# Expert weights of a mixture-of-experts step in 4 MB instead of 2 MB transfers

## Chip, core and metric

The kernel runs on one core of one Trainium2 chip. The metric is the device time of one execution in microseconds (us); the median of several executions is compared. MB in the names of transfers stands for 1,024 KB; the profile's GB/s are powers of ten.

## What is computed

One layer of a hybrid decoder on 272 prompt tokens (16 of them learned) and 8 decode tokens: a Mamba-2 group and a convolution group share an input and an output projection, and a top-4-of-32 expert block follows. Only the expert block matters here. All is float32. Cut to this part:

```python
logits = (xf @ w_router + b_router).astype(F32)
top_val, top_idx = lax.top_k(logits, TOP_K)                # 4 of 32 experts per token
gates = jax.nn.softmax(top_val, axis=-1).astype(u.dtype)
...
def expert_rows(args):
    xblk, e = args
    gt = jnp.minimum(xblk @ w_gate[e] + b_gate[e], SWIGLU_LIMIT)
    up = jnp.clip(xblk @ w_up[e] + b_up[e], -SWIGLU_LIMIT, SWIGLU_LIMIT)
    hdn = (up + 1.0) * gt * jax.nn.sigmoid(gt * SWIGLU_ALPHA)
    return hdn @ w_down[e] + b_down[e]
```

Each of `w_gate[e]`, `w_up[e]` and `w_down[e]` is 1024 x 1024 float32, 4 MB; an expert has 12 MB, the 32 experts 384 MB, and each matrix is read once. The expert block serves 264 tokens with 4 experts each, so an expert has 33 tokens in the mean.

## The kernel before

The first 286 us or so do everything ahead of the experts. Then the 32 experts are worked through in an order found at run time by their token counts: experts 0 and 1 in straight code, 2 to 31 in a loop of 15 rounds, each with a **big** and a **small** expert (`big_expert`, `small_expert`). In this text an expert's number is its place in that order; the even ones are big, the odd ones small. A big expert puts 64 tokens across TensorE's columns (line 1447, matmuls of 128 x 64 by 512), a small one has at most 32 tokens, four groups of columns (line 1490, by 256). A big expert with more than 64 tokens is done in two halves (`by_width` picks `what(2)`), so that each product is made twice; such an expert is called **wide** here.

The weights lie in a ring in SBUF of 12 pieces (`ring`, `piece(p)`), 1 MB each: pieces 0 to 3 are the gate matrix, 4 to 7 the up matrix, 8 to 11 the down matrix. The ring holds exactly one expert. On each expert TensorE goes through the pieces in this order; between them it puts the former expert's rows into the result (`scatter`, `scatter_s`), gathers the next expert's rows (`gather`, line 1424, or `gather_s`) and turns the hidden values (line 1205). Every product of a piece begins with `pe.wait_ge(landed[p // 2], i16)`: `landed` has one semaphore for each pair of pieces.

SyncE (SP) only issues transfers. The first expert's six pairs are fetched ahead (`prefetch`). Then a loop over the 31 others (lines 357 to 364) asks for pair after pair of the next expert, each as soon as TensorE has used the same pair of the present one. TensorE says so by semaphores: `gate_half` and `gate_used` for pairs 0 and 1, and `piece_used` for the others, eight counts for each expert: the fourth comes when the up matrix has been used (on a big expert by the first matmul of the gathering), the eighth at the end of the down matrix. A transfer of a pair is 128 partitions x 16 KB. All requests stand in one queue and are served in their order.

On a big expert of one width `gate_half` and `gate_used` both come with the first matmuls of piece 4; on a wide one after pieces 1 and 3 of the second half; on a small one after piece 1 and with the first matmul of piece 4.

Of the kernel before, what the change touches and what calls it, by code (L numbers as in the profile page):

```python
# [47 lines left out]
def build(nc, I, O):  # L48
    ctx = ExitStack()
    with ctx:  # L50
        def sb(name, n, dt=F32):
            return ctx.enter_context(nc.sbuf_tensor(name, [P, n], dt))

        def sem(name):
            return ctx.enter_context(nc.semaphore(name))

        def view(t, off, *dims):
            n = 1
            for d in dims:
                n *= d  # L60
            a = t[:, off:off + n]
            if len(dims) == 1:
                return a
            names = "abc"[:len(dims)]
            return a.rearrange("p (" + " ".join(names) + ") -> p " + " ".join(names),
                               **dict(zip(names, dims)))
# [12 lines left out]
        PIECE = 2 * D  # L79
        NP = 12  # L80
        ring = sb("ring", NP * PIECE)
# [131 lines left out]
        ev = {n: sem(n) for n in names}  # L213
        landed = [sem(f"pair_landed{i}") for i in range(NP // 2)]
# [28 lines left out]
        def piece(p):  # L243
            return view(ring, p * PIECE, 2, D)

        def pair_row(q):
            return view(ring, 2 * q * PIECE, 2 * PIECE)
# [4 lines left out]
        expert_w = I["w_experts"]  # L252

        def expert_pair(e, q):
            return expert_w[bass.ds(e, 1), q].rearrange("o p n -> p (o n)")

        tok = [(0, P), (P, P), (2 * P, NB)]

        NR = CW - 1
# [6 lines left out]
        def _(sp):  # L266
# [89 lines left out]
            sp.wait_ge(ev["order_ready"], 1)  # L356
            with sp.Fori(0, NE - 1) as i:
                e = sp.value_load(order[0:1, bass.ds(i + 2, 1)], min_val=0, max_val=NE - 1)
                for q in range(2):
                    sp.wait_ge(ev[("gate_half", "gate_used")[q]], i + 1)  # L360
                    sp.dma_start(pair_row(q), expert_pair(e, q)).then_inc(landed[q], 16)
                for q in range(2, NP // 2):
                    sp.wait_ge(ev["piece_used"], i * 8 + 2 * q - 2)
                    sp.dma_start(pair_row(q), expert_pair(e, q)).then_inc(landed[q], 16)

            sp.wait_ge(ev["o_tab"], 1)
            n_over = sp.value_load(otab[0:1, OVER:OVER + 1], min_val=0, max_val=OVER)
            with sp.If(n_over > 0):
                sp.wait_ge(ev["o_list"], 1)
                with sp.Fori(0, OVER) as j:  # L370
                    with sp.If(j < n_over):
                        e = sp.value_load(otab[0:1, bass.ds(j, 1)], min_val=0, max_val=NE - 1)
                        sp.wait_ge(ev["piece_used"], j * 8 + NE * 8)
                        for q in range(NP // 2):
                            sp.dma_start(pair_row(q), expert_pair(e, q)).then_inc(landed[q], 16)
            for q in range(4):
                sp.wait_ge(ev["f_ready"], 2 * q + 2)
                sp.dma_start(O["y_t"][:, 2 * TN * q:2 * TN * (q + 1)], flat(yo[:, 2 * q:2 * q + 2, :])).then_inc(ev["f_out"], 16)
# [821 lines left out]
        def _(pe):  # L1200
# [214 lines left out]
            def halves(bank):  # L1415

                return [ps[HALF * h:HALF * (h + 1), bank, :] for h in range(2)]
# [17 lines left out]
            def bias(bank, row):  # L1435
                for h_, dst in enumerate(halves(bank)):
                    MM(dst, oh[row:row + NE, :], brow[row:row + NE, 512 * h_:512 * (h_ + 1)],  # L1437
                       start=True, stop=False, skip_group_check=True)

            def piece_products(p, b, src, bank, fresh, i16):  # L1440
                pe.wait_ge(landed[p // 2], i16)
                hs = []
                for k in range(2):
                    kk = 2 * (p % 4) + k
                    o = 512 * b + P * (kk % 4) + HALF * (kk // 4)
                    for h_, dst in enumerate(halves(bank + b)):
                        hs.append(MM(dst, src[:, o:o + HALF], piece(p)[:, k, 512 * h_:512 * (h_ + 1)],  # L1447
                                     start=(fresh and kk == 0), stop=(kk == KT - 1), skip_group_check=True))
                return hs
# [11 lines left out]
            def quarters(bank):  # L1461

                return [ps[QUAR * q:QUAR * (q + 1), bank, 0:256] for q in range(4)]
# [17 lines left out]
                       start=False, stop=False, skip_group_check=True)  # L1481

            def piece_products_s(p, src, bank, fresh, i16):
                pe.wait_ge(landed[p // 2], i16)
                hs = []
                for k in range(2):
                    kk = 2 * (p % 4) + k
                    o = P * (kk % 2) + QUAR * (kk // 2)
                    for q, dst in enumerate(quarters(bank)):
                        hs.append(MM(dst, src[:, o:o + QUAR], piece(p)[:, k, 256 * q:256 * (q + 1)],  # L1490
                                     start=(fresh and kk == 0), stop=(kk == KT - 1), skip_group_check=True))
                return hs
# [71 lines left out]
            def gate_of(n, i16, then):  # L1564
                for p in range(4):
                    hs = piece_products(p, 0, xT, 0, False, i16)
                    if p == 3:
                        hs[-1].then_inc(ev["gate_done"], 1)
                    then(n, p)

            def up_of(n, i16):
                if n == 1:
                    for p in range(4, 8):
                        hs = piece_products(p, 0, xT, 2, False, i16)
                        if p == 4:
                            hs[0].then_inc(ev["gate_half"], 1)
                            hs[1].then_inc(ev["gate_used"], 1)
                        hs[-1].then_inc(ev["up_first" if p == 7 else "piece_used"], 1)
                else:
                    bias(1, 64)  # L1580
                    bias(3, 96)
                    for p in range(4):
                        hs = piece_products(p, 1, xT, 0, False, i16)
                        if p % 2:
                            hs[-1].then_inc(ev[("gate_half", "gate_used")[p // 2]], 1)
                    for p in range(4, 8):
                        hs = piece_products(p, 0, xT, 2, False, i16)
                    hs[-1].then_inc(ev["up_first"], 1)
                    for p in range(4, 8):
                        hs = piece_products(p, 1, xT, 2, False, i16)  # L1590
                        if p < 7:
                            hs[-1].then_inc(ev["piece_used"], 1)
# [19 lines left out]
            def gate_s(i16, then):  # L1612
                for p in range(4):
                    hs = piece_products_s(p, xT, 0, True, i16)
                    if p == 0:
                        bias_s(0, 64)
                    if p == 1:
                        hs[-1].then_inc(ev["gate_half"], 1)
                    if p == 3:
                        hs[-1].then_inc(ev["gate_done"], 1)  # L1620
                    then(p)

            def up_s(i16):
                for p in range(4, 8):
                    hs = piece_products_s(p, xT, 2, True, i16)
                    if p == 4:
                        hs[0].then_inc(ev["gate_used"], 1)
                        bias_s(2, 96)
                    hs[-1].then_inc(ev["piece_used"], 1)

            def down_s(i2, i16):
                pe.wait_ge(ev["ht_ready"], i2 + 2)
                pe.wait_ge(ev["xg_out"], i2 + 3)
                for p in range(8, NP):
                    hs = piece_products_s(p, hT_e, 4, True, i16)
                    hs[-1].then_inc(ev["piece_used"], 1)
# [69 lines left out]
            for m in range(4):  # L1706
                if m == 3:
                    pe.wait_ge(ev["acc_done"], NE * 4 + 1)
                for h_ in range(2):
                    q = m // 2 + 2 * h_  # L1710
# [91 lines left out]
```

## Time and profile before

| | |
|---|---|
| median of 3 runs | 1286.16 us (1285.48 to 1294.58) |
| the profiled execution | 1288.3 us, span 1286.5 us |
| TensorE matmul busy | 1173.8 us, 91% of the span |
| VectorE, ScalarE busy | 485.5 us, 195.5 us |
| mean granted TensorE clock | 0.964 of full |
| transfers | 451.33 MB, mean 351 GB/s over the span |
| weights in the loop and ahead of it | 192 transfers of 2,048 KB |

The span is cut into 40 slices of 32.2 us in the page's second part; its DMA row gives the mean busy share of the 16 DMA engines. In a timeline a row is a run of like instructions: start, length, engine, line, operation, tiles, shapes, count, and in brackets the idle time ahead of it with what ended it. SPq rows are the moments at which SP issues a transfer, not the transfer.

### The profile page before, as it was taken

To read this page: it belongs to the slowest core of one execution; us is meant where nothing else is said; L and a number is where in the kernel's file an instruction comes from. 1 tells how busy PE (TensorE), PEld (TensorE's weight loads), DVE (VectorE), ACT (ScalarE), POOL (GpSimd) and SP (SyncE) were. 2 spreads that over 40 slices of the span, in tenths; PEclk is the share of its full clock that TensorE was granted. 3 is DMA by queue.
4 is the path that set the end of the run, shared out by engine and by line. 5 is a ranking of instruction groups with operands and counts; after the bars stand their busy time and mean duration, and the time that the engine had idled before them with its cause. 6 is when DMAs were issued, how large, how long until landed. Compare 5 with 4: busy or idle time off the path is not lost.

```text
span 1286.5 us, 21155 instructions
## 1 busy us (share of the span) xinstructions
PE 1173.8 (91%) x8454; PEld 551.2 (43%) x8455; DVE 485.5 (38%) x1078; ACT 195.5 (15%) x431; POOL 4.6 (0%) x28
## 2 busy tenths in 40 slices
PE   7999989997988989999989999799998887989886
PEld 5888768873333233433333433233432322333323
DVE  2799998114432322232312233222233332323233
ACT  1234504021110110111101111100111111011012
POOL 0000000000000000000000000000000000000000
PEclk9999998997999989999989999999999999899897
DMA  9452329623999999899999899998999999999993
GB/s 396 165 208 74 139 104 318 264 74 120 381 425 427 428 427 408 329 420 431 428 428 419 329 428 429 428 428 357 393 422 428 428 428 430 426 430 427 429 428 149
DMA packets 36994, 451.33 MB, mean 351 GB/s; under 512 B 5112, under 2 KB 5656, under 8 KB 10080
## 3 DMA queue, kind: packets, MB, share of 16 engines
q1 hardware_dynamic: 35344, 449.02, 84.0%
q10 hardware_dynamic: 1616, 1.82, 0.4%
q8 instruction: 25, 0.41, 0.1%
q14 instruction: 9, 0.07, 0.0%
HBM read 443.57 MB, written 7.25 MB: 350 GB/s over the span
## 4 chain that ended last, share of the span: by engine, by line
PE 55%; DMA 30%; DVE 12%; issue 1%; DVEq 1%; ACT 0%; SPq 0%; ACTq 0%
DMA ring<-in_w_experts 29%; PE ps L1447 24%; PE ps L1490 8%; DVE acts L713 5%; PE ps L1229 3%; PE ps L1331 2%; PE ps L1424 2%; PE ps L1388 2%; PE ps L1499 2%; PE ps L1457 2%; PE ps L1205 2%; DVE acts L808 1%; PE ps L1322 1%; PE ps L1437 1%; PE ps L1480 1%
## 5 line engine op out<-in xcount | busy, mean ns | idle before, releaser
L1447 PE MATMUL ps<-ring,extra 128*64 128x512 f32 x1824 | 426.3, 613 | 15.3 <-DMA ring<-in_w_experts 15.3
L1068 DVE TENSOR_TENSOR acts<-ps,acts 128x528 f32<-128x528 f32 x128 | 90.6, 708 | 409.4 <-PE ps L1499 207.0
L1447 PEld LDWEIGHTS ps<-ring,extra 128*64 128x64 f32 x1824 | 124.3, 139 | 268.6 <-issue 235.3
L1490 PE MATMUL ps<-ring,extra 128*32 128x256 f32 x3072 | 203.3, 400 | 39.3 <-DMA ring<-in_w_experts 39.3
L1490 PEld LDWEIGHTS ps<-ring,extra 128*32 128x32 f32 x3072 | 89.8, 113 | 142.3 <-DMA ring<-in_w_experts 58.7
L713 DVE SCALAR_TENSOR_TENSOR acts<-acts,small 128x256 f32<-128x256 f32 x224 | 91.3, 477 | 0.7 <-ACT acts L453 0.7
L1229 PE MATMUL ps<-acts,ring 128*128 128x280 f32 (+1 forms) x320 | 75.3, 395 | 0.3 <-ACT ring L524 0.3
L1229 PEld LDWEIGHTS ps<-acts,ring 128*128 128x128 f32 x320 | 60.6, 190 | 14.0 <-issue 1.0
L1229 PE MATMUL ps<-acts,extra 128*128 128x280 f32 x256 | 64.2, 415 | 1.9 <-DVE acts L695 1.9
L1082 DVE TENSOR_SCALAR extra<-ps 128x512 f32<-128x512 f32 x32 | 22.0, 688 | 97.8 <-PE ps L1447 82.5
L1229 PEld LDWEIGHTS ps<-acts,extra 128*128 128x128 f32 x256 | 50.6, 198 | 14.9 <-issue 2.3
L604 ACT ACTIVATE extra<-extra 128x512 f32<-128x512 f32 x32 | 19.7, 630 | 243.7 <-DVE extra L1073 243.7
L1424 PE MATMUL ps<-acts 128*64 128x512 f32 (+1 forms) x228 | 56.6, 616 | 0.0
L1205 PE MATMUL ps<-small,extra 128*128 128x128 f32 x220 | 39.0, 290 | 14.4 <-DVE extra L1087 13.0
L1457 PE MATMUL ps<-acts,extra 64*128 64x264 f32 x304 | 51.2, 427 | 0.0
L1499 PE MATMUL ps<-acts,extra 32*128 32x264 f32 x256 | 46.7, 442 | 0.0
L1105 DVE SCALAR_TENSOR_TENSOR acts<-ps,acts 128x264 f32<-128x264 f32 x48 | 22.2, 490 | 63.3 <-ACT acts L634 63.2
L1205 PEld LDWEIGHTS ps<-small,extra 128*128 128x128 f32 x220 | 22.8, 140 | 48.6 <-issue 20.8
L1499 PEld LDWEIGHTS ps<-acts,extra 32*128 32x128 f32 x256 | 19.6, 187 | 55.8 <-issue 55.8
L599 ACT ACTIVATE extra<-ps 128x512 f32<-128x512 f32 x34 | 20.4, 600 | 144.5 <-PE ps L1424 134.2
L1055 DVE TENSOR_SCALAR extra<-ps 128x256 f32<-128x256 f32 x16 | 6.8, 425 | 83.7 <-PE ps L1490 83.7
L614 ACT ACTIVATE extra<-ps 128x512 f32<-128x512 f32 x32 | 17.4, 594 | 132.8 <-PE ps L1447 132.8
(290 smaller groups left out, 883.3 us busy)
## 6 DMA issues: line engine op xcount, KB each, us to landing
ring<-in_w_experts SPq DMA_DIRECT2D x192, 2048.0 KB, 22.1
ring<-in_w_in_t SPq DMA_DIRECT2D x5, 2048.0 KB, 20.8
extra<-in_w_in_t SPq DMA_DIRECT2D x4, 2048.0 KB, 9.3
extra<-in_w_out_t SPq DMA_DIRECT2D x4, 1024.0 KB, 5.9
ring<-in_w_out_t SPq DMA_DIRECT2D x4, 1024.0 KB, 5.8
ring<-in_state_t SPq DMA_DIRECT2D x8, 512.0 KB, 6.9
ring<-dtx_rows SPq DMA_DIRECT2D x8, 512.0 KB, 5.8
out_ssm_s_t<-ring SPq DMA_DIRECT2D x8, 512.0 KB, 4.1
```

The source lines that it names most:

```text
L713: STT(conv[:, m, 0:SEQ], cbuf[:, m, k:k + SEQ], cw[:, m, k:k + 1], conv[:, m, 0:SEQ], ALU.mult, ALU.add).then_inc(ev["tap_added"], 1)
L1068: TT(both, ps[:, 6:8, 0:TN], both, ALU.add).then_inc(ev["acc_done"], 1)
L1105: return STT(Pm[:, bank, :], ps[:, 6, 0:TN], slot_id[:, slot:slot + 1], gp, ALU.is_equal, ALU.mult)
L1205: return nc.tensor.transpose(out, in_, ident[0:r, 0:r])
L1229: h = MM(ps[:, tile_bank(j), 0:T - lo], win(c)[:, k, P * q:P * (q + 1)], uT[:, k, lo:T], start=(k == 0), stop=(k == KT - 1))
L1331: h = MM(ps[:, m, 0:TN], wout(4 + k // 2)[:, k % 2, P * m:P * (m + 1)], conv[:, k, :], start=(k == 0), stop=False, skip_group_check=True)
L1388: h = MM(ps[:, m, 0:TN], wout(k // 2)[:, k % 2, P * m:P * (m + 1)], yT[:, k, :], start=False, stop=(k == KT - 1), skip_group_check=True)
L1424: h = MM(dst, S[0:r, j, HALF * b:HALF * (b + 1)], xn[0:r, j, 512 * h_:512 * (h_ + 1)], start=(j == 0), stop=(j == 2))
L1447: hs.append(MM(dst, src[:, o:o + HALF], piece(p)[:, k, 512 * h_:512 * (h_ + 1)], start=(fresh and kk == 0), stop=(kk == KT - 1), skip_grou ...
L1457: h = MM(ps[:, 6 + h_, 0:TN], ys[rows, 512 * b + P * m:512 * b + P * (m + 1)], Pm[rows, b, :], start=(b == 0), stop=(b == n - 1))
L1490: hs.append(MM(dst, src[:, o:o + QUAR], piece(p)[:, k, 256 * q:256 * (q + 1)], start=(fresh and kk == 0), stop=(kk == KT - 1), skip_group_ ...
L1499: h = MM(ps[:, 6 + h_, 0:TN], ys[QUAR * q:QUAR * (q + 1), P * (m % 2):P * (m % 2 + 1)], Pm[QUAR * q:QUAR * (q + 1), 0, :], start=True, sto ...
```

## The change

The loop on SP asks for a whole matrix: one transfer of 128 partitions x 2 x 16 KB in place of two of 128 x 16 KB. The gate matrix is asked for at `gate_used`, the up matrix at the fourth and the down matrix at the eighth count of `piece_used`. The semaphore of the matrix's second pair (`landed[1]`, `landed[3]`, `landed[5]`) counts its landing, and TensorE waits for it ahead of the matrix's first piece only (`p % 4 == 0`). The first expert, fetched ahead by pairs as before, is still waited for by pairs. The overflow loop, which runs only if an expert's tokens don't fit, is changed in the same way; it is not entered with this data.

```diff
+        def matrix_rows(t):
+            return ring[:, 4 * t * PIECE:4 * (t + 1) * PIECE].rearrange("p (q n) -> p q n", q=2)
+
+        def expert_matrix(e, t):
+            return expert_w[bass.ds(e, 1), 2 * t:2 * t + 2].rearrange("o q p n -> p (o q) n")
...
                 e = sp.value_load(order[0:1, bass.ds(i + 2, 1)], min_val=0, max_val=NE - 1)
-                for q in range(2):
-                    sp.wait_ge(ev[("gate_half", "gate_used")[q]], i + 1)
-                    sp.dma_start(pair_row(q), expert_pair(e, q)).then_inc(landed[q], 16)
-                for q in range(2, NP // 2):
-                    sp.wait_ge(ev["piece_used"], i * 8 + 2 * q - 2)
-                    sp.dma_start(pair_row(q), expert_pair(e, q)).then_inc(landed[q], 16)
+                sp.wait_ge(ev["gate_used"], i + 1)
+                sp.dma_start(matrix_rows(0), expert_matrix(e, 0)).then_inc(landed[1], 16)
+                for t in range(1, 3):
+                    sp.wait_ge(ev["piece_used"], i * 8 + 4 * t)
+                    sp.dma_start(matrix_rows(t), expert_matrix(e, t)).then_inc(landed[2 * t + 1], 16)
...
+            def matrix_here(p, i16):
+                if isinstance(i16, int) and i16 == 16:
+                    pe.wait_ge(landed[p // 2], 16)
+                elif p % 4 == 0:
+                    pe.wait_ge(landed[p // 4 * 2 + 1], i16)
+
             def piece_products(p, b, src, bank, fresh, i16):
-                pe.wait_ge(landed[p // 2], i16)
+                matrix_here(p, i16)
```

`piece_products_s` changes like `piece_products`. The order of SP's instructions in one round of its loop, before (line 361 asks for pairs 0 and 1, line 364 for pairs 2 to 5):

```order
56 L361 ISA [waits gate_half]
57 L361 DMA ring<-in_w_experts 128x4096
58 L361 ISA [waits gate_used]
59 L361 DMA ring<-in_w_experts 128x4096
60 L363 ISA
61 L364 ISA [waits piece_used]
62 L364 DMA ring<-in_w_experts 128x4096
63 L363 REGISTER_ALU
64 L364 ISA [waits piece_used]
65 L364 DMA ring<-in_w_experts 128x4096
```

(and two more such requests behind these), and with the change (line 366 asks for the gate matrix, line 369 for the other two):

```order
56 L366 ISA [waits gate_used]
57 L366 DMA ring<-in_w_experts 128x2x4096
58 L368 ISA
59 L369 ISA [waits piece_used]
60 L369 DMA ring<-in_w_experts 128x2x4096
61 L368 REGISTER_ALU
62 L369 ISA [waits piece_used]
63 L369 DMA ring<-in_w_experts 128x2x4096
```

Six requests with a wait each have become three; the wait on `gate_half` is gone and pair 0 goes with pair 1.

On TensorE, the start of the small expert in the loop, before (line 1490 are its products, 1480 its biases, 1457 the former expert's rows; `pair_landed0` to `pair_landed5` are the semaphores in `landed`):

```order
358 L1490 MATMUL ps<-ring,extra 32x256 [waits pair_landed0]
359 L1490 MATMUL ps<-ring,extra 32x256 x7
360 L1480 MATMUL ps<-acts 32x256 x4
361 L1457 MATMUL ps<-acts,extra 128x264 [waits y_back,p_ready]
362 L1457 MATMUL ps<-acts,extra 128x264
363 L1490 MATMUL ps<-ring,extra 32x256 [waits pair_landed0]
364 L1490 MATMUL ps<-ring,extra 32x256 x7
365 L1457 MATMUL ps<-acts,extra 128x264 [waits acc_done]
366 L1457 MATMUL ps<-acts,extra 128x264
367 L1490 MATMUL ps<-ring,extra 32x256 [waits pair_landed1]
368 L1490 MATMUL ps<-ring,extra 32x256 x7
```

and with the change (the same lines are 1501, 1491 and 1468 there):

```order
358 L1501 MATMUL ps<-ring,extra 32x256 [waits pair_landed1]
359 L1501 MATMUL ps<-ring,extra 32x256 x7
360 L1491 MATMUL ps<-acts 32x256 x4
361 L1468 MATMUL ps<-acts,extra 128x264 [waits y_back,p_ready]
362 L1468 MATMUL ps<-acts,extra 128x264
363 L1501 MATMUL ps<-ring,extra 32x256 x8
364 L1468 MATMUL ps<-acts,extra 128x264 [waits acc_done]
365 L1468 MATMUL ps<-acts,extra 128x264
366 L1501 MATMUL ps<-ring,extra 32x256 x8
```

No matmul has moved; the wait for the second pair now stands ahead of the first piece, and the waits inside the matrix are gone.

## Rows read from the trace of the kernel before

**Rows 1.** The page, chain that ended last, by line.

```profile
DMA ring<-in_w_experts 29%; PE ps L1447 24%; PE ps L1490 8%; DVE acts L713 5%; PE ps L1229 3%; PE ps L1331 2%; PE ps L1424 2%; PE ps L1388 2%; PE ps L1499 2%; PE ps L1457 2%; PE ps L1205 2%; DVE acts L808 1%; PE ps L1322 1%; PE ps L1437 1%; PE ps L1480 1%
```

**Rows 2.** The page: GB/s by slice; issues with count, KB, us to landing.

```profile
GB/s 396 165 208 74 139 104 318 264 74 120 381 425 427 428 427 408 329 420 431 428 428 419 329 428 429 428 428 357 393 422 428 428 428 430 426 430 427 429 428 149
...
ring<-in_w_experts SPq DMA_DIRECT2D x192, 2048.0 KB, 22.1
```

**Rows 3.** Windows: length, busy PE PEld DVE ACT POOL, clock, DMA share, GB/s.

```profile
689.80:737.30 47.50, 46.78 (x388) 18.52 (x388) 12.01 (x25) 5.11 (x11) 0.00 (x0) 1.00 0.89 354
...
606.60:665.30 58.70, 52.51 (x404) 18.79 (x408) 17.00 (x34) 6.23 (x13) 0.00 (x0) 0.94 1.01 429
```

**Rows 4.** Timeline, experts 10 and 11; last, a request on SP and its landing.

```profile
606.66 1.94 PE L1447 MATMUL ps<-ring,extra 128*64 128x512 f32 x8 [0.63 <-DMA ring<-in_w_experts]
...
640.93 1.07 PE L1490 MATMUL ps<-ring,extra 128*32 128x256 f32 x16 [0.97 <-DMA ring<-in_w_experts]
...
636.22 0.33 SPq L364 DMA_DIRECT2D ring<-in_w_experts  x1
...
DMA to landing us min/median/max: 24.3/24.3/24.3
```

**Rows 5.** Timeline of TensorE around the wide experts (6, 12, 18).

```profile
494.44 20.82 PE L1447 MATMUL ps<-ring,extra 128*64 128x512 f32 x96
...
667.88 1.94 PE L1447 MATMUL ps<-ring,extra 128*64 128x512 f32 x8
...
735.73 3.66 PE L1490 MATMUL ps<-ring,extra 128*32 128x256 f32 x64
...
741.10 1.94 PE L1447 MATMUL ps<-ring,extra 128*64 128x512 f32 x8
...
863.29 20.82 PE L1447 MATMUL ps<-ring,extra 128*64 128x512 f32 x96
```

**Rows 6.** SP's requests around expert 12; a landing time belongs to the row above.

```profile
646.62 0.33 SPq L361 DMA_DIRECT2D ring<-in_w_experts  x1
...
DMA to landing us min/median/max: 23.6/23.6/23.6
...
666.37 0.33 SPq L364 DMA_DIRECT2D ring<-in_w_experts  x1
...
DMA to landing us min/median/max: 23.5/23.5/23.5
...
686.22 0.33 SPq L361 DMA_DIRECT2D ring<-in_w_experts  x1
...
700.48 0.33 SPq L364 DMA_DIRECT2D ring<-in_w_experts  x1
...
718.32 0.33 SPq L364 DMA_DIRECT2D ring<-in_w_experts  x1
...
DMA to landing us min/median/max: 7.8/7.8/7.8
...
727.81 0.33 SPq L361 DMA_DIRECT2D ring<-in_w_experts  x1
...
DMA to landing us min/median/max: 9.4/9.4/9.4
```

**Rows 7.** Timeline, last expert: TensorE; last request on SP and its landing.

```profile
1255.29 3.43 PE L1490 MATMUL ps<-ring,extra 128*32 128x256 f32 x32 [2.26 <-DMA ring<-in_w_experts]
...
1263.08 3.90 PE L1490 MATMUL ps<-ring,extra 128*32 128x256 f32 x64
...
1240.81 0.33 SPq L364 DMA_DIRECT2D ring<-in_w_experts  x1
...
DMA to landing us min/median/max: 24.2/24.2/24.2
```

**Rows 8.** The loop's first two requests on SP and the landings of the two.

```profile
323.33 0.94 SPq L361 DMA_DIRECT2D ring<-in_w_experts  x2
...
DMA to landing us min/median/max: 9.2/11.3/13.5
```

More of the change, by code:

```diff
@@ L373, in _ @@
                         sp.wait_ge(ev["piece_used"], j * 8 + NE * 8)
-                        for q in range(NP // 2):
-                            sp.dma_start(pair_row(q), expert_pair(e, q)).then_inc(landed[q], 16)
+                        for t in range(3):
+                            sp.dma_start(matrix_rows(t), expert_matrix(e, t)).then_inc(landed[2 * t + 1], 16)
             for q in range(4):
@@ L1483, in piece_products_s @@
             def piece_products_s(p, src, bank, fresh, i16):
-                pe.wait_ge(landed[p // 2], i16)
+                matrix_here(p, i16)
                 hs = []
```

## The prediction, made before the changed kernel ran

> **What bounds the kernel now.** I read the page's chain first, to see who ends the span. Its two largest parts are the wait for expert weights and the products that use them [rows 1]. The reader is to see that both stand side by side: the kernel is neither plainly transfer-bound nor plainly TensorE-bound. The page's slices and its table of issues come next [rows 2]: from the twelfth slice to the last but one the transfers run at 419 GB/s or more, except for three dents (408 and 329, 329, 357 and 393). There are 192 weight transfers of 2,048 KB, and a median of 22.1 us passes from request to landing, although 2 MB at 428 GB/s take 4.9 us. So most requests stand in a queue behind some 17 us of other transfers.
>
> The windows tell the two sorts of stretch apart [rows 3]. From 606.60 to 665.30, one big and one small expert, the 16 DMA engines are busy for the whole time at 429 GB/s and TensorE for 52.5 of 58.7 us: here the transfers set the pace. From 689.80 to 737.30 the rate is 354 GB/s, while TensorE is busy for 46.8 of 47.5 us: here TensorE sets it and the queue runs dry. The timeline of TensorE says why [rows 4, 5]. In a steady pair it waits before piece 0 of a big expert (606.66, 0.63 us) and before pairs of the small one (640.93, 0.97 us). An expert with more than 64 tokens takes every product twice; its row is the run of 96 matmul instructions of 20.82 us, and there are three such rows, the first at 494.44, the second at 678.94, the last at 863.29. These three wide experts (6, 12 and 18 in the order of use) make the three dents. Behind each, the transfers catch up, and TensorE waits for weights again before the next one comes (606.66 lies between the first and the second). From then on the transfers set the pace: **what the DMA engines lose around a wide expert is lost for the whole kernel.**
>
> **What the change does there.** The ring holds exactly one expert, so a transfer can start only where something was used up. The 12 MB come in three requests instead of six. The bytes, the 16 KB runs and the matmul instructions stay. Two things get coarser: a matrix is requested when its last pair is free (the first pair waits for the second), and its first product waits for 4 MB (the first pair's user waits for the second pair too).
>
> **Steady stretches cost nothing.** A 4 MB transfer takes 9.8 us. TensorE starts a matrix up to 4.9 us later than now, but then finds all of it. The gate matrix of expert 12 is the tightest to follow: its second pair is requested at 646.62 [rows 6], so at 651.5 at the latest after the change. It is needed when expert 11's last pair has landed, 636.22 + 24.3 = 660.5 [rows 4]. That is 9.0 us ahead, and a request needs 2.9 us of its own with no transfer in front of it (7.8 - 4.9, the request at 718.32 [rows 6]). So the queue does not run dry. The fewer DMA instructions on SP and fewer waits on TensorE are worth nothing here: each SP issue takes 0.33 us behind a queue of 17 us. Of cover there is 9.0 - 2.9 = 6.1 us; a stall beyond this would be lost in each pair.
>
> **Around a wide expert it costs 7.3 us.** I follow expert 12. TensorE starts it at 667.88 [rows 5] while the second gate pair lands at 646.62 + 23.6 = 670.2 [rows 6]; afterwards it starts at 670.3, 2.4 us later, and so do its releases. Before it, the down matrix of expert 12 lands last, at 689.9 (the request at 666.37 took 23.5 us [rows 6]). With 2.9 us from request to start on an idle queue and 9.8 us for 4 MB:
> - Gate of 13: requested at 686.22 + 2.4 = 688.6, starts at 691.5, lands at 701.3. Idle 1.6 us.
> - Up of 13: 700.48 + 2.4 = 702.9, starts at 705.8, lands at 715.6. Idle 4.5 us.
> - Down of 13: 718.32 + 2.4 = 720.7, starts at 723.6, lands at 733.4. Idle 8.0 us.
> - Gate of 14: 727.81 + 2.4 = 730.2, while another transfer runs. For such a request the rows show up to 9.4 us in all [rows 6], 4.5 above the transfer itself. By 4.5 it starts at 734.7 and lands at 744.5 (by 2.9 at 743.2).
>
> Before the change the second gate pair of 14 landed at 727.81 + 9.4 = 737.2. So the transfers are 7.3 us behind (6.0 by the lower price). The reason in a sentence: one expert's three requests fall 14 and 18 us apart here while a transfer lasts 9.8 us, so the engines idle between them, where the small requests in between used to fill in. Expert 13 does not wait for weights: it needs its down matrix at 735.73 + 2.4 = 738.1, and the matrix is there at 733.4. Expert 14 wants to begin at 741.10 + 2.4 = 743.5 [rows 5] and waits 1.0 us. The three wide experts have the same neighbours, a small one after them: 3 x 7.3 = 21.9 us.
>
> **Start and end.** The first request of the loop goes out with the second pair's (323.33, two in 0.94 us; the second pair lands 13.5 us after its own request, at 337.4 [rows 8]). One 4 MB request at 323.9 lands at 336.6: 0.8 us gained, hidden, but carried into the first transfer-bound stretch. At the end the last pair lands at 1240.81 + 24.2 = 1265.0 and the last product ends at 1263.08 + 3.90 = 1267.0 [rows 7], 2.0 us later, since two pieces were done before. With the whole down matrix landing at once, all 64 instructions come after it, 3.66 us in the row at 735.73 [rows 5]: 1.7 us lost. What follows the last expert does not change.
>
> **Sum**: 21.9 - 0.8 + 1.7 = 22.8 us. The profiled execution took 1288.3 us (span 1286.5), 2.1 above the median of 1286.16; I add the sum to the median: 1309.0 us, 1.8% slower.
>
> **A rule of the Trainium skill against the row.** In the stretch 606.60:665.30 twelve 2 MB transfers follow each other with the engines fully busy at 429 GB/s [rows 3]: a larger transfer finds nothing between transfers to save. The Trainium skill (DMA: Bandwidth & Descriptors, section Bandwidth) gives 341 GB/s for 1 MB and 425 GB/s for 16 MB, so larger requests should be faster; an estimate between them on a log scale gives 362 and 383 GB/s for 2 and 4 MB, 5.5% off some 910 us of transfers, about 50 us gained, and the sum would be near 1259 us. This trace has 2 MB at more than the page's rate for 16 MB, since its requests are queued.
>
> **Rivals.**
> 1. *Faster, by cheaper transfers.* Each transfer would have to carry a cost that the rows don't show. The change removes 93 requests of the loop; to end 1% under 1286 (12.9 us) against the 22.8 of the sum, each must give back 0.38 us of DMA time. Time at that point: 1273 us. Against it stands the full business of the engines [rows 3]. Chance 0.03.
> 2. *Within 1%, the loss is absorbed.* If TensorE set the pace from one wide expert to the next, later transfers would be covered, and start and end alone (0.9 us) would remain: 1287 us. It decides where less than 4 us per wide expert reach the steady stretches. For it speaks that TensorE is busy for 46.8 of 47.5 us behind expert 12; against it the wait at 606.66 [rows 4], and that a pair needs 52.5 us of TensorE and 58.7 of transfers. Chance 0.07.
> 3. *The 4 MB transfer is slower.* Each DMA engine would now step between two places of the same partition's data 2 MB apart. The trace shows no transfer of this shape. Of some 910 us of transfers each per cent of rate costs 9 us: 4% would give 1345 us. It is bounded from one side by the 12 transfers at 429 GB/s, which go through the same places one after the other. The Trainium skill (DMA: Bandwidth & Descriptors, section Latency and other measured facts) lists row pitches of 512 KiB at 207 GB/s and 2 MiB at 164; no row here shows it, and here the rows of one pair stay 16 KB apart. Chance 0.06.
> 4. *The clock of TensorE.* Waits become fewer and longer (up to 4.9 us more at a time), and after a wait of 2.26 us the granted clock's lower level (1.2 GHz) shows: 32 matmul instructions take 3.43 us at 1255.29, where 64 take 3.66 at 735.73 [rows 7, 5], 1.6 us lost. One such loss at the start of each wide expert and at the end gives 4 x 1.6 = 6.4 us more, 1315 us. In steady pairs two more fit into the 6.2 us that TensorE has to spare; only beyond it the pace changes hands. The Trainium skill (TensorE: Matmul & The Clock Gate, section HAM oscillation — how this bites in real kernels) describes matmuls that start cold after each wait for a transfer; the row agrees, with 3.43 us for 32. Chance 0.04 that it adds over 6 us.
>
> **How the numbers follow.** The forecast as worked out gets 0.80. Its low end: 6.0 instead of 7.3 for each wide expert (-3.9), and if TensorE enters them undelayed, because the transfers run 2.4 us further ahead by then, up to 4 us less: 1301. Its high end: the clock (+6.4) and half a per cent of transfer rate (+4.5): 1320. The range 1301 to 1320 leaves the rivals 1 to 3 out. A difference under about 1% can't be told from none for this kernel; slower by over 1% (above 1299) takes the forecast, rivals 3 and 4: 0.90; within 1% 0.07; faster 0.03.
>
> **What would show it.** In the profile after: 93 transfers of 4,096 KB beside the first expert's six of 2,048 KB, at 428 GB/s in steady stretches; the dents around the three wide experts deeper, with idle DMA stretches of about 1.6, 4.5 and 8 us; no idle DMA elsewhere in the expert stage; TensorE waiting once or twice in a matrix's place, for up to 4.4 us, and never inside a matrix; the last weights landing some 21 us later and the last product 3.7 us after them. A steady rate under 425 GB/s would prove rival 3; dents in steady stretches would mean that the 6.1 us of cover is not there; a start of the small expert behind a wide one that waits for weights would make each wide expert dearer than 7.3 us.

## The result, and the profile after

The changed kernel takes 1311.61 us in the median (1310.45 to 1321.4, 3 runs) against 1286.16 us: ratio 1.0206, 95% interval 1.0153 to 1.0259. By the medians it is slower by 25.5 us; the two profiled executions differ by 23.3 us (1311.6 and 1288.3 us; spans 1309.8 and 1286.5 us). The forecast was 1309.0, range 1301 to 1320. One execution of the run called wait below (1315.2 us) fell in a slower state of the chip and is left out of its median and ratio.

The page after, its slices (TensorE's granted clock in tenths, DMA share in tenths, GB/s) and its two kinds of weight requests:

```profile
PEclk9999998998989989999999998999998989898897
DMA  9451338622999997799998799997899999999992
GB/s 397 177 189 65 137 143 308 273 98 83 427 427 425 428 428 310 314 428 431 426 431 341 316 426 430 428 429 294 367 430 428 429 428 428 429 428 429 428 429 120
...
ring<-in_w_experts SPq DMA_DIRECT2D x93, 4096.0 KB, 18.8
...
ring<-in_w_experts SPq DMA_DIRECT2D x6, 2048.0 KB, 12.5
```

The three dents are where they were [rows 2] and deeper: 310 and 314 where 408 and 329 stood, 341 and 316 for 419 and 329, 294 and 367 for 357 and 393. Between them the rate is the old one. The windows say the same: a steady pair, and the stretch from the landing of expert 12's down matrix to that of expert 14's gate matrix (columns as in [rows 3]):

```profile
612.00:671.00 59.00, 52.14 (x404) 18.58 (x396) 16.09 (x33) 6.62 (x14) 0.00 (x0) 0.96 1.01 430
...
697.50:751.70 54.20, 52.36 (x440) 20.56 (x436) 12.46 (x25) 5.50 (x13) 0.00 (x0) 1.00 0.78 320
```

54.2 us, in which four transfers of 9.8 us were made: 15 us more than they take by themselves. The requests on SP in this stretch, with the time to landing behind each (gate of 13, up of 13, down of 13, gate of 14):

```profile
696.40 0.38 SPq L366 DMA_DIRECT2D ring<-in_w_experts  x1
...
DMA to landing us min/median/max: 12.1/12.1/12.1
...
710.56 0.37 SPq L369 DMA_DIRECT2D ring<-in_w_experts  x1
...
DMA to landing us min/median/max: 12.2/12.2/12.2
...
728.40 0.37 SPq L369 DMA_DIRECT2D ring<-in_w_experts  x1
...
DMA to landing us min/median/max: 12.4/12.4/12.4
...
737.99 0.38 SPq L366 DMA_DIRECT2D ring<-in_w_experts  x1
...
DMA to landing us min/median/max: 13.6/13.6/13.6
```

They land at 708.5, 722.8, 740.8 and 751.6. The gaps between requests, 14.2 and 17.8 us, are longer than a transfer of 9.8, so the queue is empty when the second and the third come, as the prediction had it.

From the landing times of all requests I worked out, for each run below, how long the DMA engines had no weights to move around each wide expert. I call it idle time: the distance between two landings less the steady time of one transfer, summed over the requests of the small expert behind the wide one and those of the next big one. It includes the time from a request on an empty queue to the start of its transfer. I also give the time from the loop's first request to the last landing, because the part of the program ahead of it varies from run to run (the first request falls between 320.6 and 330.4 us in the kernels whose big experts are not all wide).

| kernel | median, us | first request to last landing | last landing to last product | idle around the three wide experts |
|---|---|---|---|---|
| before | 1286.2 | 941.7 | 2.0 | 8.4, 8.3, 8.3 |
| after | 1311.6 | 962.0 | 5.5 | 17.0, 15.0, 14.6 |
| late | 1297.5 | 950.5 | 2.0 | 12.6, 10.9, 11.1 |
| wait | 1301.2 | 950.3 | 4.4 | 11.1, 10.8, 11.3 |
| down4 | 1297.2 | 945.1 | 5.5 | 9.7, 9.7, 9.7 |
| narrow_b | 1261.2 | 914.6 | 2.0 | no wide expert |
| narrow_a | 1263.1 | 914.6 | 5.5 | no wide expert |
| ones | 1291.0 | 943.9 | 1.1 | 3.5, 5.6, 2.9 |
| ones_down | 1282.9 | 941.2 | 1.8 | 5.8, 10.1, 4.4 |
| rows8 | 1325.6 (1 run) | 974.6 | 5.8 | 14.1, 17.3, 13.8 |

The names of the runs are explained below. Each trace is of one execution, and not always a typical one: late's was the slowest of its ten (1302.7 us), wait's among the fastest (1297.2). The kernel before ran again beside the others: 1285.4 us beside the first four experiments, 1285.2 beside the next, 1288.0 beside the last two.

### The profile page after: what moved, and what is told of

Its sections match the earlier page's. It is cut to its first block, busy times and chain, and to the rows that moved or that the text cites. A ratio compares the mean times of both kernels' runs of the same rounds, so it can differ in the third digit from the quotient of the medians.

```text
span 1309.8 us, 20814 instructions
## 1 busy us (share of the span) xinstructions
PE 1192.0 (91%) x8454; PEld 560.8 (43%) x8455; DVE 485.6 (37%) x1078; ACT 195.5 (15%) x431; POOL 4.6 (0%) x28
## 4 chain that ended last, share of the span: by engine, by line
PE 56%; DMA 29%; DVE 11%; issue 2%; DVEq 1%; ACT 0%; SPq 0%; ACTq 0%
DMA ring<-in_w_experts 28%; PE ps L1458 28%; PE ps L1501 6%; DVE acts L718 5%; PE ps L1510 3%; PE ps L1234 3%; PE ps L1336 2%; PE ps L1393 2%; PE ps L1468 2%; PE ps L1429 2%; PE ps L1210 1%; DVE acts L813 1%; PE ps L1327 1%; PE ps L1442 1%; PE ps L1749 1%
## 5 line engine op out<-in xcount | busy, mean ns | idle before, releaser
L1458 PE MATMUL ps<-ring,extra 128*64 128x512 f32 x1824 | 436.3, 626 | 27.6 <-DMA ring<-in_w_experts 27.6
L1501 PE MATMUL ps<-ring,extra 128*32 128x256 f32 x3072 | 208.5, 413 | 32.2 <-DMA ring<-in_w_experts 27.6
L1501 PEld LDWEIGHTS ps<-ring,extra 128*32 128x32 f32 x3072 | 96.6, 117 | 135.8 <-issue 61.9
L1234 PEld LDWEIGHTS ps<-acts,ring 128*128 128x128 f32 x320 | 60.5, 190 | 14.2 <-issue 1.0
L1510 PE MATMUL ps<-acts,extra 32*128 32x264 f32 x256 | 49.5, 465 | 0.0
L1468 PEld LDWEIGHTS ps<-acts,extra 64*128 64x128 f32 x304 | 23.9, 185 | 27.0 <-DVE acts L1073 19.8
```

Source lines behind the costliest of these rows:

```text
L1234: h = MM(ps[:, tile_bank(j), 0:T - lo], win(c)[:, k, P * q:P * (q + 1)], uT[:, k, lo:T], start=(k == 0), stop=(k == KT - 1))
L1468: h = MM(ps[:, 6 + h_, 0:TN], ys[rows, 512 * b + P * m:512 * b + P * (m + 1)], Pm[rows, b, :], start=(b == 0), stop=(b == n - 1))
L1510: h = MM(ps[:, 6 + h_, 0:TN], ys[QUAR * q:QUAR * (q + 1), P * (m % 2):P * (m % 2 + 1)], Pm[QUAR * q:QUAR * (q + 1), 0, :], start=True, sto ...
```

## The experiments

Three theories were put against each other. A is the prediction's: the queue runs dry around the wide experts, since requests come later and TensorE enters them later. B: the longer waits put TensorE at its lower clock, and that costs the time. C: a transfer has a price by its size.

### Is it the later request or the longer wait? (late, wait)

Two halves of the change, each alone. **late** keeps two transfers and two waits for each matrix, and asks for both when the matrix is free:

```diff
-                for q in range(2):
-                    sp.wait_ge(ev[("gate_half", "gate_used")[q]], i + 1)
-                    sp.dma_start(pair_row(q), expert_pair(e, q)).then_inc(landed[q], 16)
-                for q in range(2, NP // 2):
-                    sp.wait_ge(ev["piece_used"], i * 8 + 2 * q - 2)
-                    sp.dma_start(pair_row(q), expert_pair(e, q)).then_inc(landed[q], 16)
+                sp.wait_ge(ev["gate_used"], i + 1)
+                for q in range(2):
+                    sp.dma_start(pair_row(q), expert_pair(e, q)).then_inc(landed[q], 16)
+                for t in range(1, 3):
+                    sp.wait_ge(ev["piece_used"], i * 8 + 4 * t)
+                    for q in (2 * t, 2 * t + 1):
+                        sp.dma_start(pair_row(q), expert_pair(e, q)).then_inc(landed[q], 16)
```

> Two transfers of 2 MB per matrix as before, each with its own semaphore, but both requested only when the whole matrix has been used, as the change does. TensorE waits pair by pair as before. Theory A (the queue runs dry around the three wide experts, since requests come later and bunched): 4.9 us for each wide expert, 13 to 15 us slower than before in all, last landing 13 to 15 us later, last product 2 us after it as before. Theory B (longer waits put TensorE at its lower clock, and that costs the time): 0 to 3 us, since its waits stay as short as before. Theory C (a 4 MB transfer is dearer in itself): 0, since none is made.

**wait** keeps the requests and changes TensorE's waits alone (the condition in `matrix_here`, cut):

```diff
+                elif p % 4 == 0:
+                    pe.wait_ge(landed[p // 2], i16)
+                    pe.wait_ge(landed[p // 2 + 1], i16)
```

> Requests by pairs of 2 MB at the old moments; only TensorE's wait is changed: ahead of a matrix's first piece it waits for both pairs. Theory A: the wide experts start 2.4 us later and everything they release with them, 3 x 2.4 = 7.2 us at the last landing, and 1.7 to 3.4 us more at the end, since the whole down matrix is multiplied after its landing: 9 to 11 us slower than before. Theory B: nearly the whole 23 us, since all the long waits of the change are there. Theory C: 0.

Measured: late 1.0079 of the kernel before (1.0052 to 1.0107), 10 us; wait 1.0098 (1.0059 to 1.0137), 13 us. Each half costs by itself, so neither theory B nor theory C can be the whole: late still waits pair by pair (its longest wait for weights is 2.7 us, against 2.4 before and 4.3 in the changed kernel), and neither has a transfer over 2 MB. In the traces the last landing comes 8.8 us (late) and 8.7 us (wait) later, measured from the first request, and wait loses 2.4 us more at its end. wait's 11.1 us in the trace fit the 9 to 11 expected; the 13 us of its runs are above, with an interval from 7.6 to 17.6 us. The two halves add up to 17.5 us at the last landing, where the whole change has 20.3.

late fell short of its 13 to 15 us. Two rows show a part of the reason. In the kernel before, the last pair of expert 11's up matrix, right ahead of wide expert 12, is multiplied at the lower clock (1.2 GHz, half of the higher one); the same instructions in late, ahead of the same expert, run at the higher one. Before (timeline of TensorE):

```profile
647.39 1.94 PE L1490 MATMUL ps<-ring,extra 128*32 128x256 f32 x16
650.72 3.64 PE L1490 MATMUL ps<-ring,extra 128*32 128x256 f32 x32 [1.40 <-DMA ring<-in_w_experts]
```

late:

```profile
661.88 1.93 PE L1491 MATMUL ps<-ring,extra 128*32 128x256 f32 x32 [2.25 <-DMA ring<-in_w_experts]
...
677.31 1.94 PE L1448 MATMUL ps<-ring,extra 128*64 128x512 f32 x8
```

32 instructions in 3.64 us against 1.93. The kernel before starts expert 12 at 667.88 [rows 5], 2.5 us after its first pair has landed; late starts it 0.8 us after. With an entry 1.7 us earlier the requests come earlier too, and the idle time ahead of expert 13's up matrix is 1.8 us, where at the first wide expert, which late entered 2.1 us behind its first pair, it is 3.2. There the whole idle time is 12.6 us, close to the 13.2 that the expectation implies (8.3 + 4.9). So the kernel before itself holds 1.6 to 1.7 us of slow clock ahead of each wide expert (32 instructions in 3.64, 3.64 and 3.56 us), which my expectation took for fixed work. It also goes some way to explain why the halves add up to less than the whole: the early entries helped late at experts 12 and 18, and the changed kernel, which must wait for the whole gate matrix, can't have them. No run separates this from other effects of the two halves on each other.

The length of the wait does not decide the clock here. In the kernel before it had fallen ahead of the wait of 1.40 us (16 instructions in 1.94 us at 647.39, where 16 take 1.07 at 640.93 [rows 4]), and late kept the higher clock behind a wait of 2.25 us, but had the lower one behind a wait of 2.27 us ahead of expert 6:

```profile
473.10 3.29 PE L1491 MATMUL ps<-ring,extra 128*32 128x256 f32 x32 [2.27 <-DMA ring<-in_w_experts]
```

### Is it the wide experts? (narrow_b, narrow_a)

The same edit in both kernels takes the wide experts away. It leaves out the second half of the products of the three experts with more than 64 tokens, so both kernels do less work than the layer asks for, and the same less:

```diff
-                with pe.If(count < HALF + 1):
+                with pe.If(count < TN + 1):
```

> The kernel before, with the width taken as one half for every expert (the comparison in by_width against 65 becomes one against 265): the second half of the three experts with more than 64 tokens is left out. Theory A: with no wide expert the transfers never stop, and the 8.3 us of idle DMA time around each of the three are gone: 25 us faster than the kernel before, near 1261 us, rate 428 GB/s in every slice of the expert stage. It is the base for narrow_a.

> The changed kernel with the width taken as one half for every expert: the same second halves are left out as in narrow_b. Theory A: what is left of the change is the start (-0.8 us) and the end (+1.7 to 3.4 us), so 1 to 3 us slower than narrow_b, near 1263 us. Theory B (TensorE's clock after long waits): most of the 23 us between the two remains, since the waits of the steady stretches are all there. Theory C (a 4 MB transfer is dearer): about 20 us between the two.

Measured: 1261.2 us (1257.2 to 1263.8, 4 runs) and 1263.1 us (1261.7 to 1274.5, 4 runs). Of the change's 25 us, 1.9 are left by the medians of four runs each, whose ranges overlap; by the traces, counted from the first request, it is 3.5 us, all of it at the end. From the first request to the last landing both take 914.6 us: in steady stretches 4 MB transfers on late requests cost nothing that the trace shows. The two pages' DMA rows have no dent, narrow_b first:

```profile
DMA  9451329613699999999999999999999999999993
```

narrow_a:

```profile
DMA  9551329623799999999999999999999999999992
```

This shows where the time goes. Theory B is out as the main cause, although its mechanism is there: narrow_a's mean clock is 0.935 and narrow_b's 0.952, the matmuls of line 1458 are busy for 386.6 us where line 1447 has 375.4, and none of it reaches the last landing, since the transfers set the pace. In these two kernels the clock costs time only behind the last landing (below).

### Is the loss at the wide expert or in what follows it? (wide_b, wide_a)

The opposite edit makes both halves for every big expert, so that transfers never have to catch up:

```diff
-                with pe.If(count < HALF + 1):
+                with pe.If(count < 0):
```

> The kernel before, with both halves made for every big expert (the comparison in by_width is never true), so TensorE sets the pace everywhere and transfers wait for it. Base for wide_a. Near 1576 us: 13 more wide experts at some 22 us each.

> The changed kernel with both halves made for every big expert. Theory A: idle DMA time at each of the 16 wide experts is never turned into waiting, since the transfers never have to catch up; the same time as wide_b within 3 us. If each wide expert cost 7 us wherever it stood (loss at the wide expert itself and not in the stretch behind it), it would be over 100 us slower than wide_b. Theory C: the same as wide_b too.

Measured: 1571.5 us (1568.0 to 1575.6) and 1569.6 us (1563.6 to 1583.2), the same within their spread. In the traces the time from the loop's first request to the last product is 1221.6 and 1221.4 us; the profiled execution of wide_a (1583.2 us) is longer mainly because its loop began 14.6 us later. Around the wide experts wide_a has the long idle gaps (3.8, 4.2 and 9.8 us for expert 13's three matrices), and nothing waits for them: no weights are waited for on TensorE, which is busy for 96% of the span in both. The line of the costliest group of wide_a (columns as in the page's fifth part: busy, mean ns, idle before):

```profile
L1458 PE MATMUL ps<-ring,extra 128*64 128x512 f32 x3072 | 686.8, 600 | 0.0
```

So an idle DMA engine costs nothing where TensorE sets the pace from one wide expert to the next, and all of it where transfers must make up for it later. With three wide experts of sixteen the second holds, as the wait in [rows 4] said.

### One matrix alone (down4)

Only the down matrix in 4 MB, the others in pairs (its requests; its wait ahead of piece 8 changes with them).

```diff
+                for q in range(2, 4):
+                    sp.wait_ge(ev["piece_used"], i * 8 + 2 * q - 2)
+                    sp.dma_start(pair_row(q), expert_pair(e, q)).then_inc(landed[q], 16)
+                sp.wait_ge(ev["piece_used"], i * 8 + 8)
+                sp.dma_start(matrix_rows(2), expert_matrix(e, 2)).then_inc(landed[5], 16)
```

> Only the down matrix is requested and waited for as one 4 MB transfer; gate and up stay in pairs. Theory A: the down request comes about 7 us after the first of its two pairs did, the queue is idle for 11 to 12 us around each wide expert in place of 8.3, last landing 7 to 9 us later, the end 1.7 to 3.5 us more: 9 to 12 us slower than before, nearly half of the change by one matrix of three. Theory C: a third of the 23 us, 7 us, spread evenly over the experts and not in the three places.

Measured: 1.0115 of before (1.0066 to 1.0163); the medians are 11.9 us apart. The shape is as theory A has it: 9.7 us of idle time in one piece ahead of the down matrix of experts 7, 13 and 19, none elsewhere around them. Its size is less, 9.7 instead of 11 to 12, again with an entry into the wide expert 0.8 us after its first pair. The trace gives 3.4 us at the last landing, where 7 to 9 were expected, and 3.5 at the end, 6.9 in all, while the interval of the runs begins at 8.5 (0.66% of 1285); with four runs between 1293 and 1309 us I leave open what the rest is. What the trace shows is not spread over the experts, as theory C wanted it.

### The other direction (ones, rows8, ones_down)

**ones** requests and waits for each piece of 1 MB by itself (cut; the gate matrix's four requests stand ahead of these, two behind `gate_half` and two behind `gate_used`).

```diff
+                for p in range(4, NP):
+                    sp.wait_ge(ev["piece_used"], i * 8 + p - 3)
+                    sp.dma_start(piece_row(p), expert_piece(e, p)).then_inc(landed[p], 16)
```

> The other direction: every piece of 1 MB is requested by itself, as soon as the present semaphores tell that it is free, and waited for by itself. Theory A (what counts is how early and how evenly the requests come around the three wide experts): idle DMA time around each wide expert falls from 8.3 to 6 or 7 us, and the end gains up to 0.9 us, since three of the four last pieces are multiplied before the last lands: 4 to 6 us faster than before. Theory C (each transfer carries a cost, so larger ones are better and smaller ones worse): slower than before, by 186 more transfers times their cost. The steady rate stays at 428 GB/s by theory A.

It missed: 1.0041 of before (1.0022 to 1.0060), 5 us slower. Half of theory A held, and more than hoped: idle time around the wide experts fell from 8.3 to between 2.9 and 5.6 us, which is 13 us in all. The other half, the unchanged rate, did not hold. A long steady window, before, and the same of ones:

```profile
980.00:1250.00 270.00, 235.77 (x1854) 82.84 (x1850) 80.54 (x160) 30.11 (x64) 0.00 (x0) 0.96 1.01 428
```

ones:

```profile
980.00:1250.00 270.00, 234.48 (x1852) 81.36 (x1854) 79.96 (x160) 30.19 (x65) 0.00 (x0) 0.96 1.01 422
```

422 instead of 428 GB/s with the engines as busy as before: 2.485 us for 1 MB where half of a 2 MB transfer takes 2.448. 372 transfers times 0.037 are 14 us, which eats the gain; the last landing comes 2.2 us later than before and the end is 0.9 us shorter. These 1.3 us of the trace are less than the runs' interval (2.8 to 7.7 us), and the rest stays open.

**rows8** asks what this is the price of. It is the changed kernel, each 4 MB cut into two transfers of 2 MB with rows of 8 KB (the gate matrix's requests):

```diff
+                for h in range(2):
+                    sp.dma_start(matrix_rows(0)[:, :, h], expert_matrix(e, 0)[:, :, h]).then_inc(landed[h], 16)
```

> The changed kernel with each 4 MB transfer cut into two of 2 MB whose rows are 8 KB long (the left and the right half of each partition's two 16 KB runs), both requested at the same moment and both waited for. It tells where the 0.037 us for each MB come from. If from the row's length (8 KB rows): 4.97 us for each 2 MB in the steady stretches. If from the number of transfers: 4.90 us, as the 2 MB transfers of 16 KB rows take.

Measured: 4.971 us for each 2 MB in the steady stretch (averaged over the last ten experts), against 4.896 in the kernel before, whose transfers are as large and as many. So the price comes with the row of 8 KB and not with the number or the size of the transfers. In ones and in rows8 alike a row of 8 KB is also half of a 16 KB run, with the other half left out between rows; no run tells the length of a row from this gap. The one execution of rows8 took 1325.6 us. Its window:

```profile
1010.00:1290.00 280.00, 244.16 (x1894) 88.95 (x1894) 81.98 (x163) 30.53 (x65) 0.00 (x0) 0.93 1.01 422
```

and that of the changed kernel with its rows of 16 KB:

```profile
1000.00:1280.00 280.00, 248.51 (x1946) 90.23 (x1948) 82.33 (x164) 30.52 (x65) 0.00 (x0) 0.93 1.01 428
```

In the steady part transfers of 16 KB rows took 4.896 us for 2 MB in one transfer and 9.788 for 4 MB: the larger one saves 0.004 us. Theory C has nothing left.

**ones_down** pays this price only on the down matrix, where the longest idle time was (its requests):

```diff
+                for p in range(8, NP):
+                    sp.wait_ge(ev["piece_used"], i * 8 + p - 3)
+                    sp.dma_start(piece_row(p), expert_piece(e, p)).then_inc(landed[p], 16)
```

> Only the down matrix is requested and waited for in pieces of 1 MB; gate and up stay in pairs of 2 MB. From the run with all pieces of 1 MB: idle DMA time around a wide expert was 3.4 to 6.0 us in place of 8.3, but each 1 MB transfer took 2.485 us where half of a 2 MB one takes 2.448. Theory A with this price: 3 x 3 us gained around the wide experts, 124 x 0.037 = 4.6 us lost, 0.9 us gained at the end: 3 to 7 us faster than before. If the small transfers' price holds and they gain nothing around the wide experts, 4 us slower.

Measured: 1282.9 us, 0.997 of before (0.9949 to 0.9991), 3.9 us faster. By its runs this version beats both kernels, though by little: the gain is within the expected 3 to 7 us, and its interval ends just short of 1. The one profiled execution shows only 0.6 us of it behind the loop's first request (0.5 at the last landing, 0.1 at the end): 4.7 us less idle time around the wide experts, and 124 x 0.037 = 4.6 us more for the small rows. Around the second wide expert, which TensorE entered 4.0 us after its first pair landed, it still had 10.1 us, against 5.8 and 4.4 at the others (entered 2.2 and 0.7 us after). So the gain is measured, but that it comes about as expected is not shown.

## Why the prediction was right

**What bounds the kernel** held: the steady stretches run at the transfers' rate, the three wide experts at TensorE's, and what is lost around them stays lost. The narrow and the wide kernels show both conditions of it, each by taking the other stretch away.

**Steady stretches cost nothing** held: 914.6 us in both narrow kernels.

**7.3 us for each wide expert**: the three requests were counted to start after 1.6, 4.5 and 8.0 us of idle time and the gate matrix of 14 after 1.3. Expert 13 showed 1.3, 4.5, 8.3 and 1.0; 15.0 in all against 15.4. The three places lost 8.6, 6.7 and 6.3 us more than before, 21.6 against 21.9. The first was dearer: TensorE began wide expert 6 at 486.3, 1.5 us after its gate matrix had landed, where it began 12 and 18 within 0.1 us of the landing. Ahead of it 48 instructions had run at the lower clock (2.80 us at the higher one, at 1276.77; mean granted clock 0.85 from 463 to 486):

```profile
467.48 5.35 PE L1501 MATMUL ps<-ring,extra 128*32 128x256 f32 x48
```

The 2.9 us from request to start were read from a request that did not quite find the queue empty: the one before it, at 711.46, landed at 719.2, 0.9 us after 718.32. The two requests of the changed kernel that did find it empty (710.56 and 728.40) needed 2.4 and 2.6 us beyond the 9.8 of the transfer, so this error is small.

**Start**: 0.8 us to be gained, 0.7 measured (337.4 - 323.3 before, 336.3 - 322.9 after). Between the three places the kernel before had lost 0.6 us once (at expert 21), which the changed one did not lose. 21.6 - 0.7 - 0.6 gives the 20.3 us at the last landing. That the sum came so close is in part luck: the first wide expert was 1.3 us dearer than counted, the other two 1.6 us cheaper together, and the 0.6 us took back a part of what the end, below, was counted too low.

**The end was sized too low.** 1.7 us were counted for multiplying the whole down matrix after its landing; 3.5 were measured. The term was mis-sized by the row that priced it: 64 instructions at the higher clock, 3.66 us. After the wait they ran at the lower one (last request, its landing, and the last products):

```profile
1266.65 0.37 SPq L369 DMA_DIRECT2D ring<-in_w_experts  x1
...
DMA to landing us min/median/max: 18.3/18.3/18.3
...
1285.06 5.33 PE L1501 MATMUL ps<-ring,extra 128*32 128x256 f32 x64 [1.07 <-DMA ring<-in_w_experts]
```

5.33 us instead of 3.66. Rival 4 had this price (1.6 us) and got a chance of 0.04 for over 6 us in all; here the clock added some 3 us, 1.8 at the end and 1.3 at the first wide expert. narrow_a and down4 ended in the same way (5.34 and 5.35 us). wait came to its last products 0.7 us after their landing, without a wait, and had them in 3.66. The Trainium skill (TensorE: Matmul & The Clock Gate, section HAM oscillation — how this bites in real kernels) describes a kernel whose matmuls start cold behind each wait for a transfer. The row at 1285.06 agrees; late's row at 661.88, at the higher clock behind a wait of 2.25 us, shows that here not every wait has this effect.

**Rival 1**, that larger transfers are cheaper, is out by 9.788 us for 4 MB against twice 4.896. **Rival 2**, the absorbed loss, does occur in another kernel: wide_a. **Rival 3**, the slower 4 MB transfer, is out at 428 GB/s. The slow row pitches that the Trainium skill (DMA: Bandwidth & Descriptors, section Latency and other measured facts) lists are steps from partition to partition. Here that step stays 16 KB, only the two runs of one partition lie 2 MB apart, and the rate is the old one.

**What was to be seen after**: the 93 and 6 requests, the three dents, the gaps of 1.6, 4.5 and 8 us came as said; elsewhere the largest idle time is 1.2 us, ahead of expert 3, where the kernel before has 1.5. The last product came 5.5 us after the last landing, not 3.7. TensorE's waits got fewer and longer, as expected (28 instead of 41, the longest 4.3 instead of 2.4 us). The prediction says nothing of their sum; one would think that it grows with the time. It did not: 55.2 us against 54.6. In TensorE's own account the time shows as matmuls at the lower clock: its busy time rose from 1173.8 to 1192.0 us, 18.2 of the 23.3. That is where the time shows, not what caused it: around the wide experts, where it is lost, the clock is 1.00 (697.50 to 751.70), and in narrow_a the slower matmuls cost nothing up to the last landing. A row from the changed kernel's steady stretch, at the start of expert 10, where the kernel before has 1.94 us for the same 8 instructions [rows 4]:

```profile
619.19 3.44 PE L1458 MATMUL ps<-ring,extra 128*64 128x512 f32 x8 [2.73 <-DMA ring<-in_w_experts]
```

So in the steady stretches slower matmuls fill time that would otherwise show as waiting, and the sum of the waits is too small a measure of the room that TensorE has.

## What to carry to other kernels

In this kernel, where a ring holds one unit of work and a queue feeds it, the size of a request (2 or 4 MB) did not matter in stretches where the queue was never empty, and mattered in full where the consumer fell behind for once and the transfers had to catch up afterwards. In a kernel like it, look for the slow exceptions and write down the requests around them against the time of one transfer. Smaller requests there are worth having only while their rows stay long: here the step from rows of 16 KB to 8 KB cost 1.5% of the rate, as much as the finer requests brought. If the end of a stage waits for its last data, price it at TensorE's lower clock too: the three kernels that waited for a whole last matrix (after, narrow_a, down4) all had it there.

## What the runs showed that I had not expected

- Rows of 8 KB move at 422 GB/s, rows of 16 KB at 428, in requests of 2 MB each and with fully busy engines (4.971 against 4.896 us). The 8 KB rows also skip 8 KB between them.
- The busy time of TensorE can grow by 18 us with the same instructions, while its waits stay the same, when the waits get longer: the mean granted clock went from 0.964 to 0.946.
- The kernel before already loses 1.6 to 1.7 us ahead of each wide expert by the lower clock. The length of the wait ahead does not tell when: late had the same 32 instructions in 1.93 us behind a wait of 2.25 us and in 3.29 us behind one of 2.27.
- The moment of the loop's first request varies by 10 us between traces of kernels that are alike up to it (320.6 to 330.4). That is much of the distance between the fastest and the slowest run of one kernel (1283.3 to 1297.8 us beside the first four experiments), though with one trace of each kernel it isn't shown that the one makes the other. It is the reason why the stages were compared from that request on.
